# Second x tile loaded and squared in parts, one gain product moved, the last half output scaled and stored in two pieces: a one-layer transformer block on one core

## What is computed

```python
def rms_norm(x, g):
    xf = x.astype(jnp.float32)
    y = xf * lax.rsqrt(jnp.mean(xf * xf, axis=-1, keepdims=True) + NORM_EPS)
    return (y * g.astype(jnp.float32)).astype(x.dtype)

    h = rms_norm(x, mix_norm_g[layer])
    proj = h @ w_in[layer]
    ...
    x = x + merged @ w_o[layer]
    h = rms_norm(x, ffn_norm_g[layer])
    x = x + (jax.nn.silu(h @ w_ffn_gate[layer]) * (h @ w_ffn_up[layer])) @ w_ffn_down[layer]
return rms_norm(x, final_norm_g)
```

## Time and profile before

| | us |
|---|---|
| median of 3 runs (lowest to highest) | 390.68 (390.55 to 391.27) |
| the profiled execution, its own time | 391.3 |
| its span, first to last instruction | 389.6 |
| PE busy in the span | 379.6 (97%) |
| DVE / ACT / POOL busy | 246.9 / 198.4 / 35.2 |

### The profile page before, as it was taken

One profiled execution on the slowest core, in us unless ns is written; L12 is line 12 of the kernel. 1 busy time (PEld: TensorE's weight loads), 2 busy tenths in 40 slices (PEclk: granted clock), 3 DMA queues, 4 the chain that ended last, 5 costly groups with the idle time before them and its releaser, 6 DMA issues.

```text
span 389.6 us, 5227 instructions
## 1 busy us (share of the span) xinstructions
PE 379.6 (97%) x2043; PEld 323.8 (83%) x2043; DVE 246.9 (63%) x326; ACT 198.4 (51%) x246; POOL 35.2 (9%) x39
## 2 busy tenths in 40 slices
PE   6999999999999999999999999999999999999993
PEld 5999888777788888888878888888888888888882
DVE  3999969548639576669547683744737366473225
ACT  4866896554584636063456463461725527163014
POOL 2698010000000010000110000000000000000002
PEclk9999999999999999999999999999999999999999
DMA  7997357835526579536336756639275481930002
GB/s 263 282 285 256 108 196 259 301 110 158 174 100 211 161 295 332 191 113 202 119 109 218 228 184 233 189 135 302 68 278 155 168 265 65 317 108 0 0 0 109
DMA packets 47369, 70.55 MB, mean 181 GB/s; under 512 B 2252, under 2 KB 30968, under 8 KB 47352
## 3 DMA queue, kind: packets, MB, share of 16 engines
q1 hardware_dynamic: 47136, 70.03, 53.8%
q10 hardware_dynamic: 216, 0.28, 0.2%
HBM read 69.26 MB, written 1.05 MB: 180 GB/s over the span
## 4 chain that ended last, share of the span: by engine, by line
PE 96%; DMA 1%; issue 1%; DVE 1%; ACT 0%; POOLq 0%; POOL 0%; SPq 0%; DVEq 0%; ACTq 0%
PE pa L1170 19%; PE pp L1179 14%; PE pp L1180 13%; PE pp L1181 13%; PE pa L1172 10%; PE pp L1170 4%; PE pp L1157 3%; PE pp L1172 2%; PE pa L1180 2%; PE pa L1179 2%; PE pa L1181 2%; DMA x_sb<-in_x 1%; PE pa L1150 1%; PE pa L1149 1%; PE pa L1148 1%; PE pa L1465 1%
## 5 line engine op out<-in xcount | busy, mean ns | idle before, releaser
L741 DVE TENSOR_TENSOR w_lo<-w_raw,w_hi 128x2048 fp32r<-128x2048 f32 x38 | 86.2, 2284 | 31.0 <-ACT w_hi L443 30.8
L443 ACT ACTIVATE w_hi<-w_raw 128x2048 fp32r<-128x2048 f32 x38 | 72.7, 1916 | 27.3 <-PE pp L1181 14.5
L1170 PE MATMUL pa<-hT,w_hi 128*128 128x512 f32 x320 | 79.9, 392 | 0.0
L1170 PEld LDWEIGHTS pa<-hT,w_hi 128*128 128x128 f32 x320 | 58.2, 189 | 10.8
L1095 DVE TENSOR_TENSOR w_lo<-w_raw,w_hi 128x2048 fp32r<-128x2048 f32 x24 | 53.6, 2287 | 8.9 <-ACT w_hi L698 8.9
L1179 PE MATMUL pp<-w_hi,hT 128*128 128x512 f32 x128 | 51.1, 400 | 0.0
L1181 PE MATMUL pp<-w_lo,hT 128*128 128x512 f32 x128 | 50.0, 390 | 0.0
L1180 PE MATMUL pp<-w_hi,hT 128*128 128x512 f32 x128 | 49.9, 390 | 0.0
L1172 PEld LDWEIGHTS pa<-hT,w_lo 128*128 128x128 f32 x320 | 43.7, 190 | 3.1
L1172 PE MATMUL pa<-hT,w_lo 128*128 128x256 f32 x320 | 44.6, 282 | 0.0
L698 ACT ACTIVATE w_hi<-w_raw 128x2048 fp32r<-128x2048 f32 x24 | 44.0, 1899 | 0.0
(11 more groups left out here) (226 smaller groups left out, 498.1 us busy)
## 6 DMA issues: line engine op xcount, KB each, us to landing
w_raw<-in_w_in SPq DMA_DIRECT2D x21, 1024.0 KB, 5.4
w_raw<-in_w_ffn_gate SPq DMA_DIRECT2D x11, 1024.0 KB, 5.4
w_raw<-in_w_ffn_up SPq DMA_DIRECT2D x11, 1024.0 KB, 6.4
w_raw<-in_w_ffn_down SPq DMA_DIRECT2D x11, 1024.0 KB, 6.7
w_raw<-in_w_o SPq DMA_DIRECT2D x4, 1024.0 KB, 6.5
w_raw<-in_w_out_attn SPq DMA_DIRECT2D x2, 1024.0 KB, 5.1
w_raw<-in_w_out_mlstm SPq DMA_DIRECT2D x2, 1024.0 KB, 5.0
x_sb<-in_x SPq DMA_DIRECT2D x2, 512.0 KB, 4.1
```

What stands on the lines that cost most here:

```text
L443: nc.scalar.activation(w_hi[:, slot_of(c), :], w_raw[:, c % RAW, :], ACT.Copy).then_inc(hi_ready, 1)
L741: nc.vector.tensor_tensor(w_lo[:, slot_of(c), :], w_raw[:, c % RAW, :], w_hi[:, slot_of(c), :].bitcast(F32), ALU.subtract).then_inc(lo_rea ...
L1170: mm(banks[:, f, :], w_hi[:, s, w[k]], hT[:, k], start=(k == 0), stop=False)
```

## The change

Three edits. (1) x tile 1 is loaded as two DMAs of 128x512 instead of one of 128x1024. ACT squares quarters 0 and 2, DVE quarters 1 and 3, each as its half arrives; DVE's second square takes the first one's sum as its start value, and one instruction adds the three sums. DVE's copy `gcol` stands between its two squares. (2) The product of the first half of tile 1 with `gain_fin` moves on DVE from behind the last sum to ahead of the last residual. (3) DVE scales the second half of tile 1 as two quarters, and SP stores each quarter by its own DMA.

```diff
--- before.py
+++ after.py
@@ -160,7 +160,8 @@
                 return pp[:, ft, 0:S]
             return pa[:, ft // 2 - 2, ft % 2 * S:(ft % 2 + 1) * S]
 
-        x_loaded = [sem(f"x_loaded{t}") for t in range(T)]
+        x_loaded = [sem(f"x_loaded{n}") for n in ("0", "1_first", "1_second")]
+        x1_partial = sem("x1_partial")
         gain_loaded = sem("gain_loaded")
         gain_turned = sem("gain_turned")
         gcol_set = sem("gcol_set")
@@ -304,7 +305,8 @@
                     sp.dma_start(as_source(w_raw[:, c % RAW, :], src), src).then_inc(chunk_loaded[c % RAW], 16)
 
             sp.dma_start(x_t[:, 0], x_d[:, 0]).then_inc(x_loaded[0], 16)
-            sp.dma_start(x_t[:, 1], x_d[:, 1]).then_inc(x_loaded[1], 16)
+            for h in range(2):
+                sp.dma_start(x_t[:, 1, HALVES[h]], x_d[:, 1, HALVES[h]]).then_inc(x_loaded[1 + h], 16)
             for c in range(C_FFN + 2):
                 load(c, chunk_source(c))
                 if c == 1:
@@ -340,11 +342,12 @@
                                      ).then_inc(chunk_loaded[slot], 16)
             c = C_FFN + 2 + 3 * (FG - 1)
             load(c, down_k[:, 2 * (FG - 1):2 * FG, :])
-            for ready, t, h in ((out00_ready, 0, 0), (out01_ready, 0, 1), (out11_ready, 1, 1)):
-                sp.wait_ge(ready, 1)
-                sp.dma_start(out_d[:, t, HALVES[h]], rb_t[:, t, HALVES[h]]).then_inc(stored, 16)
-
-            sp.wait_ge(stored, 16 * 4)
+            for ready, n, t, cols in ((out00_ready, 1, 0, HALVES[0]), (out01_ready, 1, 0, HALVES[1]),
+                                      (out11_ready, 1, 1, QUARTERS[2]), (out11_ready, 2, 1, QUARTERS[3])):
+                sp.wait_ge(ready, n)
+                sp.dma_start(out_d[:, t, cols], rb_t[:, t, cols]).then_inc(stored, 16)
+
+            sp.wait_ge(stored, 16 * 5)
 
 
         @block.gpsimd
@@ -529,12 +532,14 @@
             nc.scalar.activation(sinv[:, 0:8], minus_half[:, :], ACT.Square)
             act.dma_start(vec_rows[0:4, :], mlstm_norm_g.rearrange("a (h p) -> (a h) p", p=P)).then_inc(vec_loaded, 16)
             act.dma_start(vec_rows[4:36, :], conv_qk.rearrange("a j (f p) -> (a j f) p", p=P)).then_inc(vec_loaded, 16)
-            for t in range(T):
-                act.wait_ge(x_loaded[t], 16)
-                if t:
-                    act.wait_ge(square_act, 1)
-                nc.scalar.activation(o_sb[:, 0:512], x_t[:, t, HALVES[0]], ACT.Square, scale=D ** -0.5,
-                                     accum_out=sumsq[:, 2 * t:2 * t + 1]).then_inc(square_act, 1)
+            act.wait_ge(x_loaded[0], 16)
+            nc.scalar.activation(o_sb[:, 0:512], x_t[:, 0, HALVES[0]], ACT.Square, scale=D ** -0.5,
+                                 accum_out=sumsq[:, 0:1]).then_inc(square_act, 1)
+            for h in range(2):
+                act.wait_ge(x_loaded[1 + h], 16)
+                act.wait_ge(square_act, 1 + h)
+                nc.scalar.activation(o_sb[:, 0:256], x_t[:, 1, QUARTERS[2 * h]], ACT.Square, scale=D ** -0.5,
+                                     accum_out=sumsq[:, 2 + h:3 + h]).then_inc(square_act, 1)
             norm_half1(0)
             act.wait_ge(gcol_set, 1)
             xT_hi(0)
@@ -874,19 +879,28 @@
                                                in1=hT_hi[:, k, :].bitcast(F32), op0=ALU.mult, op1=ALU.subtract
                                                ).then_inc(hT_lo_set, 1)
 
-            for t in range(T):
-                if t:
-                    dve.wait_ge(gain_turned, 1)
-                    nc.vector.tensor_copy(gcol[:, :], pa[:, 3, 0:KT]).then_inc(gcol_set, 1)
-                    dve.wait_ge(square_dve, 1)
-                dve.wait_ge(x_loaded[t], 16)
-                nc.vector.tensor_tensor_reduce(
-                    out=o_sb[:, 512:1024], in0=x_t[:, t, HALVES[1]], in1=x_t[:, t, HALVES[1]], scale=1.0 / D,
-                    scalar=EPS, op0=ALU.mult, op1=ALU.add, accum_out=meansq[:, t:t + 1]).then_inc(square_dve, 1)
-                dve.wait_ge(square_act, t + 1)
-                dve.wait_ge(square_dve, t + 1)
-                nc.vector.tensor_tensor(meansq[:, t:t + 1], meansq[:, t:t + 1], sumsq[:, 2 * t:2 * t + 1], ALU.add
-                                        ).then_inc(meansq_set, 1)
+            dve.wait_ge(x_loaded[0], 16)
+            nc.vector.tensor_tensor_reduce(
+                out=o_sb[:, 512:1024], in0=x_t[:, 0, HALVES[1]], in1=x_t[:, 0, HALVES[1]], scale=1.0 / D,
+                scalar=EPS, op0=ALU.mult, op1=ALU.add, accum_out=meansq[:, 0:1]).then_inc(square_dve, 1)
+            dve.wait_ge(square_act, 1)
+            dve.wait_ge(square_dve, 1)
+            nc.vector.tensor_tensor(meansq[:, 0:1], meansq[:, 0:1], sumsq[:, 0:1], ALU.add).then_inc(meansq_set, 1)
+            dve.wait_ge(x_loaded[1], 16)
+            nc.vector.tensor_tensor_reduce(
+                out=o_sb[:, 512:768], in0=x_t[:, 1, QUARTERS[1]], in1=x_t[:, 1, QUARTERS[1]], scale=1.0 / D,
+                scalar=EPS, op0=ALU.mult, op1=ALU.add, accum_out=meansq[:, 2:3]).then_inc(x1_partial, 1)
+            dve.wait_ge(gain_turned, 1)
+            nc.vector.tensor_copy(gcol[:, :], pa[:, 3, 0:KT]).then_inc(gcol_set, 1)
+            dve.wait_ge(x1_partial, 1)
+            dve.wait_ge(x_loaded[2], 16)
+            nc.vector.tensor_tensor_reduce(
+                out=o_sb[:, 768:1024], in0=x_t[:, 1, QUARTERS[3]], in1=x_t[:, 1, QUARTERS[3]], scale=1.0 / D,
+                scalar=meansq[:, 2:3], op0=ALU.mult, op1=ALU.add, accum_out=meansq[:, 1:2]).then_inc(square_dve, 1)
+            dve.wait_ge(square_act, 3)
+            dve.wait_ge(square_dve, 2)
+            nc.vector.scalar_tensor_tensor(out=meansq[:, 1:2], in0=sumsq[:, 2:3], scalar=sumsq[:, 3:4],
+                                           in1=meansq[:, 1:2], op0=ALU.add, op1=ALU.add).then_inc(meansq_set, 1)
             dve.wait_ge(rstd_done, 1)
             nc.vector.tensor_scalar(rb_t[:, 0, HALVES[0]], x_t[:, 0, HALVES[0]], rstd[:, 0:1], None, ALU.mult
                                     ).then_inc(half0_normed, 1)
@@ -1114,6 +1128,9 @@
             out_meansq(0, 2, sumsq[:, 8:9], sumsq[:, 9:10])
             residual(1, 1, pp[:, 3, :], ffn_out_done, 4, x3_part_done)
 
+            dve.wait_ge(x3_done[2], 1)
+            nc.vector.tensor_tensor(rb_t[:, 1, HALVES[0]], x_t[:, 1, HALVES[0]], gain_fin[:, HALVES[0]], ALU.mult
+                                    ).then_inc(gained[2], 1)
             last = (slice(None), 1, QUARTERS[3])
             dve.wait_ge(x3_part_done, 1)
             dve.wait_ge(ffn_out_done, 5)
@@ -1125,12 +1142,11 @@
                 op0=ALU.mult, op1=ALU.add, accum_out=meansq[:, 5:6]).then_inc(x3_rest_square, 1)
             dve.wait_ge(x3_rest_square, 1)
             out_meansq(1, 4, sumsq[:, 11:12], meansq[:, 5:6])
-            nc.vector.tensor_tensor(rb_t[:, 1, HALVES[0]], x_t[:, 1, HALVES[0]], gain_fin[:, HALVES[0]], ALU.mult
-                                    ).then_inc(gained[2], 1)
             dve.wait_ge(rstd_done, 6)
-            nc.vector.scalar_tensor_tensor(out=rb_t[:, 1, HALVES[1]], in0=x_t[:, 1, HALVES[1]], scalar=rstd[:, 5:6],
-                                           in1=gain_fin[:, HALVES[1]], op0=ALU.mult, op1=ALU.mult
-                                           ).then_inc(out11_ready, 1)
+            for n in (2, 3):
+                nc.vector.scalar_tensor_tensor(out=rb_t[:, 1, QUARTERS[n]], in0=x_t[:, 1, QUARTERS[n]],
+                                               scalar=rstd[:, 5:6], in1=gain_fin[:, QUARTERS[n]], op0=ALU.mult,
+                                               op1=ALU.mult).then_inc(out11_ready, 1)
 
 
         @block.tensor
```

## The result

| | before | after |
|---|---|---|
| median of 22 runs each, us | 390.61 (390.43 to 391.5) | 391.40 (390.82 to 393.3) |
| ratio, with 95% interval | | 1.0028 (1.0018 to 1.0038) |
| profiled execution, its own time / span | 391.3 / 389.6 | 393.06 / 391.5 |
| PE's first product / last product (start) | 9.78 / 382.76 | 11.73 / 384.86 |
| from PE's last product to the end of the span | 6.84 | 6.64 |

The account below looks back on a forecast made before the run. PE, busy in 97% of the span, was taken as the bound, leaving only its idle ends to shorten. Start -0.10, product -0.18 and two pieces -0.25 gave -0.53 us: 390.68 to 390.15 us, range 389.6 to 390.8.

Parts of the forecast that it names:

- the failed step: Start: SP's one extra DMA issue ahead of the weights, 0.42 us, was costed at nothing because transfers queue.
- my own sign of being wrong: Start: x's second part landing after 6.5 us would show the forecast wrong.
- The term of -0.10 us: Start, squares by quarters: PE's ninth `w_lo` product moves from 15.1 to 15.0 us, limited by the weights.
- my cover for the first square: Start: DVE's first 256-column square, some 0.6 us, fits in 1.23 us of idle time if its half lands earlier.
- The slower rival: Start: each load has its own landing pitch, PE starts 1.87 us later, 392.1 us; chance 0.07.
- my own worst sum of 391.3: Whole kernel: all bounds at their worst give +0.65 us, 391.3 us.
- Forecast -0.18: End, product moved: `rstd` ready earlier, from -0.38 us on POOL's power and +0.20 on the residual.
- The +0.20 that I took for the residual: End: moved product waits for POOL's first power, so the last residual starts 0.20 us later.
- Forecast -0.25: End, last half in two pieces: store data ends at R + 2.75 instead of R + 3.00, R being the final scaling's start.
- my 2.75: End: store data forecast to end 2.75 us behind the final scaling's start, in place of 3.00.
- The rival (same landing for each store): End: each store costs its own fixed time, so two pieces gain nothing; 390.4 us, chance 0.13.
- -0.43 forecast: End: sum of the moved product's -0.18 us and the two pieces' -0.25 us.

Follow-up runs that it names:

- E4: Kernel before with x tile 1 loaded as two column halves, both engines waiting for both and squaring 512 columns: 393.2 us, ratio 1.0046.
- E9: Kernel before with x tile 1 loaded as two DMAs of 64 partitions with 4 KB rows, squares unchanged: 392.67 us, ratio 1.0056.
- E11: Kernel before with only the product moved ahead of the last residual: 390.36 us, ratio 0.9993.
- E2: Kernel before with the product moved and the last half in two pieces, start unchanged: 390.19 us, ratio 0.9986.
- E3: Kernel before with squares by quarters but one whole load of x tile 1, end unchanged: 390.40 us, ratio 0.9993.
- E14: Kernel before with product moved, last half in two pieces, and three small loads issued behind weight chunk 2 instead of 1: 390.87 us.
- E17: Repeat of the kernel before with product moved and last half in two pieces, start unchanged: 390.35 us, ratio 0.9991.
- E12: Kernel before with only the last half scaled and stored in two pieces: 390.66 us, ratio 0.9997.
- E7: The kernel before, unchanged, profiled again: 390.78 us; its profiled run took 392.74.
- E6: The whole change with 33 warm-up turns of the identity on PE in place of 23: 391.52 us.
- E8: The whole change, unaltered, profiled again: 392.08 us; its profiled run took 392.5.
- E16: Kernel before with product moved, last half in two pieces, and whole x tile 1 on ACT's queue behind the gain rows: 393.05 us.
- E5: The whole change with x tile 1 left as one load: 390.78 us, ratio 0.9997.
- E13: The whole change with the three small loads (two biases, gate columns) issued behind weight chunk 2 instead of 1: 391.65 us.
- E15: The whole change with x tile 1's second half on ACT's queue, behind the gain rows: 390.78 us, ratio 1.0008.
- E1: Kernel before with only two loads of x tile 1 and squares by quarters, end unchanged: 391.53 us, ratio 1.0026.
- E10: The whole change with x tile 1's second half issued first on ACT's queue, ahead of the gain rows: 392.04 us.

## Why the prediction was wrong

**The start: the failed step.** I wrote: "Since the transfers queue behind each other I cost that issue at nothing", and looked for a delay only at the weights. The weights weren't pushed back by the issue: their second half lands at 10.1 us (issue 2.67 + 7.4), where it landed at 10.2 before. It is x itself that came late: by my own sign of being wrong, a second part landing after 6.5, it was at 7.36. E4 and E9 show that dividing the load is enough, whichever way it is cut. Over the profiles, ten with one load on SP's queue have landings of 5.4 to 7.2 us (median 5.6), seven with two loads 7.0 to 7.6 (median 7.3). The term of -0.10 us stands for what is in truth a delay of x by some 1.7 us. Less than that reaches the end, because with an early x the weights can set the pace: in E11's profile x lands at 5.5 but PE waits 1.0 us for the first copied weights and starts its products at 9.51, and between E2's profile and the one that I had read the first product moves by 0.97 us (8.81, 9.78) and the last by 0.78.

**The row that I built on.** The profiled execution took 0.6 us more than the median, and I noted that without asking why. Most likely it was the very term at stake: tile 1 landed at 6.25 there, in E2, E3, E11, E14 and E17 at about 5.3. No profile of the kernel before at its median was taken, so this isn't shown; E12 and E7, with the same load, have landings of 7.2 and 6.7. The 1.23 us of DVE idle time on which my cover for the first square rested is 0.30 us in E2.

**The clock.** No part of my text priced what PE's clock does if x comes later. It is half of the profiled loss: of the 1.95 us by which the first product moves, 0.98 arise between the turns' start and that product. The mean granted clock marks the same seven runs as the times do, and E6 takes them away by filling only PE's idle time. Ahead of the fall PE was idle for 2.2 to 2.7 us in all four profiles that have it (after, E4, E8, E16); with 1.4 to 1.8 us (before, E5, E9, E12, E13, E15) none has it. The fall doesn't need the change: one of 29 runs of the kernel before in E1's call took 392.74 us with a mean of 0.991. But it is more frequent with it, 7 of 22. The turns that stay slow from the start (E1, E7, E10) are something else, and no run here was made for them.

**The slower rival.** "Each load costs a landing of its own" had a chance of 0.07. Its direction was right. Its price of 1.87 us at PE, thus 392.1, is too high for most runs, and the pitch is not fixed: the two halves land 1.3 us apart, not 2.1. My range left this case out, and my own worst sum of 391.3 too.

**The product moved: right in kind, the hold one-sided as far as it shows.** Forecast -0.18; E11 measured 0.3 us less. POOL's power fell from 0.93 to 0.55 in every profile with the move. The +0.20 that I took for the residual was +0.08: DVE's product, started while POOL's first power ran for another 0.10 to 0.11 us, took no longer. By the rule that I cited (the Trainium skill, "SBUF — State Buffer", who interferes with whom) it should have been blocked until POOL was done; by these rows a DVE instruction with two SBUF inputs holds up a POOL instruction that starts behind it, and the case in the other order shows no hold. Its overlap is short, and whether POOL still read its inputs in that tenth of a microsecond isn't shown.

**Two pieces: overpriced.** Forecast -0.25; E12 shows -0.03 by medians and 0.1 in its span. The stores' data does start sooner, but it takes 3.2 us in one stretch where two pairs of halves took 2.8 in two (323 to 333 GB/s against 370). So it ends at 2.9 us behind the final scaling's start in place of my 2.75, and most of the quarter that starts sooner is used up. The rival (same landing for each store) isn't right either: the two quarters land after 1.8 and 2.5 us and ACT's half after 2.1, in place of 2.3 and 2.7. The Trainium skill's rule of about 2.0 us for each DMA plus its bytes ("DMA: Bandwidth & Descriptors", anatomy of one DMA), which is fitted on another path, would by my estimate put a 0.13 MB store at 2.3 us; the two here lie at 1.8 and 2.5, on either side of it.

**The end together: right by luck.** -0.43 forecast, -0.42 in E2's span, -0.5 by its median and -0.3 by E17's. But the parts are -0.33 and -0.1 in the spans of E11 and E12, not -0.18 and -0.25: the two misses cancel. With the squares by quarters in place the two edits at the end bring nothing in the profiles (6.43 us from the last product to the end in E3, 6.42 in E5), since 0.37 of the idle 0.44 us that the moved product fills is gone already.

**Open.** Why SP's queue moves only some 180 to 250 GB/s in a stretch that ends near 6 us, and why it reaches into tile 1 once that has two loads. So the failed step is shown, its cause isn't. It isn't the packets' size (E9), nor the small loads behind (E13). In E10 the same stretch moves 382 and 404 GB/s, so it isn't a limit of the memory or of the DMA engines as such. Why the last residual starts 0.44 us behind the end of the one before it in some kernels and 0.07 in others, with the same instructions around it, wasn't found either. It doesn't wait for PE, whose last product ended at 383.04 while the residual started at 383.51 in the kernel before. And it is the squares by quarters at the other end of the program that go with it, not the divided load: E1 and E3 have 0.75 us between the two starts, E4 and E9 1.11 and 1.12.

## What to carry to other kernels

Before costing a divided load at nothing, ask what the queue moves in just that stretch, and whether the profile read is typical there: with the same start a load's landing differed by up to 1.8 us between profiles (5.4 in E2, 7.2 in E12), and the one profile that I read was no typical one. Time in which PE waits early can have a second price, the lower clock for the work behind it, and an edit that makes the wait longer can pay it in a part of the runs; the mean granted clock of each run tells which. A DVE instruction that stands beside a POOL instruction on the path to the end is worth moving if an idle gap is near: 0.38 us freed for 0.08. And if an edit far away has closed that gap already, the move brings nothing.

## What the runs showed of the hardware

- One load of 0.5 MB cut in two, by columns or by rows, put its last landing from a median of 5.6 us (ten profiles) to 7.3 us (seven) at the program's start.
- PE idle from 6.4 to 8.9 us: granted clock 0.50 from 8.8 to 12.2, twelve turns in 2.79 us against 1.50. With turns in the gap: 1.00 from 8.8 to 12.2.
- In every profile PE's first eleven turns took 2.61 us, 0.24 each, at a clock column of 1.00; later twelve took 1.50 at the same reading.
- A POOL power of one column took 0.93 us when it started behind a DVE product of two SBUF inputs, 0.55 alone; the DVE product took 0.68 both without a POOL power in flight and with one in its first 0.11 us.
- With a store in two pieces of 0.13 MB these landed 1.8 and 2.5 us after their issue; stores of 0.26 MB landed after 2.1 to 2.7.
